# A two-layer transformer trunk on one core: the second MLP product by seven half-size products in place of eight

## The reference, cut to what matters

```python
# x: (1, 512, 1024) float32; D_FF = 4096; two layers
x = x + mixer(rmsnorm(x, g))               # attention, a different one in each layer
x = x + _mlp(rmsnorm(x, g), w1[i], w2[i])  # after each mixer
...
def _mlp(h, w1, w2):                       # w1: 1024 x 4096, w2: 4096 x 1024
    return jnp.square(jax.nn.relu(h @ w1)) @ w2
...
return _rmsnorm(x, norm_final)
```

## Time and profile before

| | |
|---|---|
| median of 3 runs | 1215.82 us (1214.65 to 1218.02) |
| the profiled execution | 1217.92 us |
| its span, first to last instruction | 1216.0 us |
| mean granted TensorE clock | 0.985 of full |
| PE busy | 96% (1166.2 us) |
| DVE, ACT, POOL busy | 56%, 42%, 43% |
| transfers | 104.94 MB, 86 GB/s on average |

### The profile page before, as it was taken

One profiled execution on the slowest core, in us unless ns is written; L12 is line 12 of the kernel. 1 busy time (PEld: TensorE's weight loads), 2 busy tenths in 40 slices (PEclk: granted clock), 3 DMA queues, 4 the chain that ended last, 5 costly groups with the idle time before them and its releaser, 6 DMA issues.

```text
span 1216.0 us, 15801 instructions
## 1 busy us (share of the span) xinstructions
PE 1166.2 (96%) x5601; PEld 959.6 (79%) x5605; DVE 678.5 (56%) x1094; ACT 505.6 (42%) x910; POOL 523.1 (43%) x267
## 2 busy tenths in 40 slices
PE   6999988999999999999997899989999999999997
PEld 4788877878888888888765677878788888888886
DVE  5867697664163163265669798737641541632654
ACT  6677665532132222225373387843322222221332
POOL 2433322444444444347643475224444444544441
PEclk9999989999999999999999999999999999999998
DMA  5233332333333333333322100103333333333331
GB/s 158 72 108 93 101 111 72 97 88 96 95 103 88 103 92 98 99 91 103 87 56 66 35 19 27 45 18 99 90 89 105 92 99 100 91 103 88 102 95 77
DMA packets 191225, 104.94 MB, mean 86 GB/s; under 512 B 9062, under 2 KB 187537, under 8 KB 191170
## 3 DMA queue, kind: packets, MB, share of 16 engines
q1 hardware_dynamic: 189900, 104.09, 29.8%
q10 hardware_dynamic: 1270, 0.13, 0.1%
HBM read 102.04 MB, written 6.35 MB: 89 GB/s over the span
## 4 chain that ended last, share of the span: by engine, by line
PE 81%; DVE 9%; ACT 5%; issue 3%; POOL 1%; DMA 1%; SPq 0%; ACTq 0%; DVEq 0%
PE bank L706 25%; PE bank L708 25%; PE bank L707 25%; ACT probs L1361 2%; PE bank L877 2%; DVE probT_l L1797 1%; POOL wl L1619 1%; PE bank L879 1%; PE bank L889 1%; ACT ur L1180 1%; PE bank L890 1%; DVE score L2118 1%; DVE probs L2020 1%; DMA score<-in_x 1%; ACT wh L1180 1%
## 5 line engine op out<-in xcount | busy, mean ns | idle before, releaser
L1619 POOL TENSOR_TENSOR wl<-raw,wh 128x1024 fp32r<-128x1024 f32 x171 | 417.9, 2445 | 549.1 <-ACT wh L1180 549.1
L706 PE MATMUL bank<-ur,wh 128*128 128x512 f32 x1072 | 418.6, 390 | 0.3 <-POOL wl L1619 0.3
L707 PE MATMUL bank<-ur,wh 128*128 128x512 f32 x1072 | 417.3, 389 | 0.0
L708 PE MATMUL bank<-ur,wl 128*128 128x512 f32 x1072 | 417.3, 389 | 0.0
L1180 ACT ACTIVATE wh<-raw 128x1024 fp32r<-128x1024 f32 x171 | 180.8, 1058 | 509.4 <-PE bank L708 509.0
L706 PEld LDWEIGHTS bank<-ur,wh 128*128 128x128 f32 x1072 | 201.5, 188 | 42.9 <-issue 1.6
L707 PEld LDWEIGHTS bank<-ur,wh 128*128 128x128 f32 x1072 | 201.4, 188 | 42.3 <-issue 0.5
L708 PEld LDWEIGHTS bank<-ur,wl 128*128 128x128 f32 x1072 | 201.4, 188 | 41.8
L1961 DVE TENSOR_TENSOR xT<-bank,xT 128x512 f32<-128x512 f32 x64 | 44.3, 692 | 227.6 <-PE bank L708 227.5
L1797 DVE TENSOR_TENSOR ur<-sq,ur 128x512 fp32r<-128x512 f32 x65 | 129.8, 1997 | 45.4 <-ACT ur L1180 45.4
L706 PE MATMUL bank<-xh,wh 128*128 128x512 f32 (+1 forms) x296 | 122.4, 413 | 8.9 <-DVE xl L1867 3.9
(11 more groups left out here) (221 smaller groups left out, 1293.7 us busy)
## 6 DMA issues: line engine op xcount, KB each, us to landing
raw<-in_w_mlp SPq DMA_DIRECT2D x128, 512.0 KB, 3.9
raw<-in_w_in_e SPq DMA_DIRECT2D x18, 512.0 KB, 3.7
raw<-in_w_in_o SPq DMA_DIRECT2D x10, 512.0 KB, 3.7
raw<-in_w_out_e SPq DMA_DIRECT2D x8, 512.0 KB, 3.8
raw<-in_w_out_o SPq DMA_DIRECT2D x8, 512.0 KB, 3.7
skew_c<-bias_rows SPq DMA_DIRECT2D x8, 319.5 KB, 4.5
strip_raw<-skew_c SPq DMA_DIRECT2D x8, 256.0 KB, 2.6
out<-probs SPq DMA_DIRECT2D x4, 512.0 KB, 2.6
```

The costliest lines, as they stand in the source:

```text
L706: mm(dst, lhs[0], rhs[0], start=start, stop=False, skip_group_check=not check)
L707: mm(dst, lhs[0], rhs[1], start=False, stop=False, skip_group_check=not check)
L708: return mm(dst, lhs[1], rhs[0], start=False, stop=stop, skip_group_check=not check)
L1619: return nc.gpsimd.tensor_tensor(dst, a, b, ALU.subtract)
```

## The change: what it does

In the first three groups of each MLP (`FAST = 3`) the second product is made by Strassen's scheme. The group's product (512 tokens x 1024 hidden features by 1024 x 1024) is cut in two in each direction. `h` gives four quarters of 512 hidden features x 256 tokens, W2 four quarters of 512x512 (`x`, `y`, `z`, where `z` is loaded twice, and each in two buffers of 128x1024). From the `h` quarters three more are made by sums and differences, so `combo_h` and `combo_l` hold seven combinations, four tiles each; the weight quarters are combined in place by four differences. Seven products of 512x512 by 512x256 follow, each of 48 matmuls with 128x128 weights and 256 moving columns. They accumulate in two pairs of banks (`z`, `v`), and after each product DVE adds the state of its pair into a quarter of `xT`. The fourth group of each layer is made as before.

The first product's slabs come in another order (tile 0, 4, 1, 5, ...), so that both halves of a pair are there early. DVE now takes a slab by one instruction (ReLU and scale, into `u_scaled`), ACT squares it, DVE makes the sums, ACT rounds the seven combinations and DVE makes their seven low parts. ACT rounds the weight combinations too, and DVE makes all their low parts. In these groups POOL only makes `wl` for the eight slabs of the first product. At the end there are four output buffers, and the transposes of features 0 to 511 stand ahead of the sum of squares.

```diff
+PRODUCTS = ((A11, "z", True, 0, "x", (0, 0)), (S1, "v", True, 1, "x", (1, 1)), (S2, "z", False, 2, "x", (0, 1)),
+            (S4, "v", False, 0, "z", (0, 1)), (S3, "z", False, 1, "y", (1, 1)), (A12, "v", True, 0, "z", (0, 0)),
+            (A22, "z", False, 1, "z", (1, 0)))
...
-        otok = praw[:, 0:2048].rearrange("p (a n) -> p a n", a=2)
+        otok = [praw[:, 0:1024], praw[:, 1024:2048], raw[:, 0, :], raw[:, 1, :]]
...  TensorE
+            def fast_group(layer, n0, norm, g):
+                G0 = FAST * layer
+                first_slabs(n0, norm, g)
+                for i, (c, pair, fresh, slot, _, _) in enumerate(PRODUCTS):
+                    pe.wait_ge(quarter_lo, HALVES * g + (HALVES * G0 + 2 * i + 2))
+                    if i < 3:
+                        pe.wait_ge(combo_lo, PARTS * g + (PARTS * G0 + (13, 15, 16)[i]))
+                    w = quarter_w[slot]
+                    for b in range(2):
+                        if i >= 2:
+                            pe.wait_ge(product_taken, BANKS_DONE * g + (BANKS_DONE * G0 + 2 * (i - 2) + b + 1))
+                        for d in range(2):
...
+                            for j in range(4):
...
+                                last = product(dst, (w[0][j // 2][:, cols], w[1][j // 2][:, cols]),
+                                               (combo_h[:, c, j, :], combo_l[:, c, j, :]), ...)
+                        last.then_inc(product_done, 1)
...
+            pe.wait_ge(slab_taken, N_END - 3)
+            pe.wait_ge(xg_hi, XG_BEFORE["final"] + 4)
+            for a in range(NQ):
+                turn_output(a, 0)
             pe.wait_ge(slab_taken, N_END)
             sum_squares("final")
...  ScalarE, group G, slab s
+                    if s + 2 < KT:
+                        split(n % 2, raw_count(n + 2), n + 1)
+                    act.wait_ge(slab_taken, n + 1)
+                    if s % 2 == 0:
+                        nc.scalar.activation(u_first[:, HS:3 * HS], u_scaled, ACT.Square).then_inc(u_ready, 1)
+                        act.wait_ge(sums_made, SUMS * G + 4 * j + 1)
+                        copy(combo_h[:, S3:A11 + 1, j, :], ...).then_inc(combo_hi, 1)
+                    else:
...  (the square, and three copies behind u_ready and sums_made)
+                    if s == 1:
+                        quarter_rounded(G, 0)
+                    if s == 4:
+                        quarter_rounded(G, 1)
...  VectorE, group G, slab s
+                    v.scalar_tensor_tensor(u_scaled, pj(n)[:, :], 0.0, rstd[:, :], ALU.max, ALU.mult).then_inc(slab_taken, 1)
+                    if s == 2:
+                        quarter_low(G, 0, 0)
+                    if s in (3, 4):
+                        quarter_sum(G, 0, s - 3)
+                    if s in (6, 7):
+                        quarter_sum(G, 1, s - 6)
+                    dve.wait_ge(u_ready, u + 1)
...  (one difference of 256 columns for even s, three for odd s)
+                    if s == 2:
+                        quarter_low(G, 0, 1)
+                    if s in (5, 6):
+                        quarter_low(G, 1, s - 5)
+                    if s == 7:
+                        quarter_sum(G, 2, 0)
...  (low parts: one of 512 columns for even s; 512, 256 and 512 for odd s)
```

More of the change, by code:

```diff
@@ L169, in trunk @@
         xT = sb("xT", [P, KT, S])
-        xh = sb("xh", [P, KT, S], F32R)
-        xl = sb("xl", [P, KT, S], F32R)
+        xhl = sb("xhl", [P, 2 * KT * S], F32R)
+        xh, xl = (xhl[:, KT * S * a:KT * S * (a + 1)].rearrange("p (k s) -> p k s", k=KT) for a in range(2))
         raw = sb("raw", [P, 2, 1024])
@@ L622, in load_mlp @@
-            def load_mlp(layer, n0):
-                with sp.Fori(0, GROUPS) as g:
-                    load_mlp_group(layer, n0, g)
+                for s in cols:
+                    n = n0 + KT * g + s
+                    sp.wait_ge(w_hi, n - 1)
+                    sp.wait_ge(w_lo, n - 1)
+                    tile = PAIR_ORDER[s] if g < FAST else s
+                    dst = raw[:, n % 2, :].rearrange("p (k n) -> p k n", k=KT)
+                    sp.dma_start(dst, w1[:, :, D * g + P * tile:D * g + P * (tile + 1)]).then_inc(raw_loaded[n % 2], 16)
@@ L779, in mlp, with turn_output, first_slabs @@
-            def mlp(n0, H0, norm):
-                mlp_group(n0, H0, norm, 0)
-                with pe.Fori(1, GROUPS) as g:
-                    mlp_group(n0, H0, norm, g)
+            def turn_output(a, half):
+                for k in range(4):
+                    last = nc.tensor.transpose(out_rows(a, half)[:, P * k:P * (k + 1)],
+                                               xT[:, 4 * half + k, P * a:P * (a + 1)], ident[:, :])
+                last.then_inc(fin_turned[half], 1)
+            def first_slabs(n0, norm, g):
+                for s in range(KT):
+                    n = KT * g + (n0 + s)
+                    pe.wait_ge(slab_taken, n - 3)
+                    wait = (lambda k: pe.wait_ge(xg_lo, XG_BEFORE[norm] + k + 1)) if s == 0 else None
+                    part = {0: lambda: sum_squares(norm), 1: lambda: spread(norm)}.get(s) if isinstance(g, int) and g == 0 else None
+                    slab(n, (n0 + s) % 2, pj(n0 + s)[:, :], xn, wait, norm_part=part, after=4 - s)
@@ new lines, in plain_group, with mlp @@
+            def plain_group(layer, n0, norm):
+                first_slabs(n0, norm, FAST)
+                for m in range(KT):
+                    n = n0 + KT * (FAST + 1) + m
+                    pe.wait_ge(slab_taken, n - 3)
+                    wait = (lambda k: pe.wait_ge(h_lo, KT * layer + k + 1)) if m == 0 else None
+                    slab(n, n % 2, pj(n)[:, :], hid, wait)
+            def mlp(layer, n0, norm):
+                fast_group(layer, n0, norm, 0)
+                with pe.Fori(1, FAST) as g:
+                    fast_group(layer, n0, norm, g)
+                plain_group(layer, n0, norm)
@@ L1305, in hidden, with quarter_rounded @@
                 copy(hid[0][:, slot, :], sq[:, slot % 2, :]).then_inc(h_hi, 1)
-            def mlp_group(n0, H0, g, norm=None, low=False):
+            def quarter_rounded(G, i):
+                _, _, _, slot, name, _ = PRODUCTS[i]
+                act.wait_ge(quarter_loaded[name], {"x": 32 * G + 32, "y": 32 * G + 32, "z": 64 * G + 32 * (1 + (i > 4))}[name])
+                made = (0, 2, 4, 0, 6, 0, 8)[i]
+                for half in range(2):
+                    if made:
+                        act.wait_ge(quarters_made, 8 * G + made - 1 + half)
+                    copy(quarter_w[slot][0][half], quarter[name][half]).then_inc(quarter_hi, 1)
@@ L1309, in mlp_group, with plain_group @@
+            def plain_group(layer, n0, norm, low):
                 for s in range(2 * KT):
-                    n = 16 * g + (n0 + s)
-                    if not isinstance(g, int) or n + 2 < N_END:
-                        split((n0 + s) % 2, raw_count(n + 2) if isinstance(g, int) else 128 * g + raw_count(n0 + s + 2),
-                              n + 1)
+                    n = n0 + KT * FAST + s
+                    if n + 2 < N_END:
+                        split(n % 2, raw_count(n + 2), n + 1)
@@ L1327, in mlp_group, with mlp @@
                                 copy(dst[0], src).then_inc(low_hi, 1)
-            def mlp(n0, H0, norm, following, low=False):
+            def mlp(layer, n0, norm, following, low=False):
                 root(norm)
-                with act.Fori(0, GROUPS - 1) as g:
-                    mlp_group(n0, H0, g)
-                mlp_group(n0, H0, GROUPS - 1, following, low)
+                for g in range(FAST):
+                    fast_group(layer, n0, g)
+                plain_group(layer, n0, following, low)
             def load_exp():
```

309 lines of the change are left out of this document (229 added, 80 removed).

## The result

The changed kernel takes 1226.34 us (median of 7 runs, 1222.36 to 1228.52) against 1218.02 us before, measured beside it: a ratio of 1.008, 95% interval 1.0063 to 1.0097.

The account below looks back on a forecast made before the run. The MLPs were taken as bound by the number and length of PE's matmuls. From 1217.9 us profiled: matmuls -26, stalls +38, clock +5, end -2 gave 1233, or 1231 in terms of the median; range 1203 to 1243.

Parts of the forecast that it names:

- rivals 2 and 3: 2: later products stall too, 1240 us, chance 0.15; 3: 256-column matmuls bound by weight load, 1330 us, chance 0.02.
- Rival 1: DVE keeps pace, so product 0's low part is ready at slab 7's end: 1188 us, half-way 1206; chance 0.2.
- Rival 4: All but nothing: 4 to 5 us of stall, no clock fall, 1213 to 1219 us; chance 0.08.
- The matmuls: Each fast group swaps 8 slabs for 336 matmuls of 256 columns at 0.1167 us, saving 4.3 us, 26 in all.
- The stalls: First half of each fast group: PE waits before slabs 4, 6, 7 and products 0, 1; 6.3 us, bounds 4.9 to 8.
- The turns of VectorE and POOL: DVE instructions with both operands in SBUF and POOL's never run side by side; if they could, stall would be 0.3 us.
- The clock: PE gaps before slab 7 and product 0 lower the clock; half of six falls at 1.7 us, +5, bounds 0 to 10.
- The second half: During the seven products DVE has 10 instructions of 1024 columns; low parts and weight quarters arrive in time, no stall.
- The end: After the last MLP, 16 early transposes and stores limited by DVE's scalings save 2 us; bounds 0 and 4.

Follow-up runs that it names:

- the kernel with short POOL instructions: Changed kernel with GpSimd making only 128 of 1024 columns of each low part of the first product's weights in the six fast groups; 1193.33 us, one run.
- the kernel with all spread anew: Changed kernel with first combinations made early for second and third groups, second combination rounded earlier, VectorE's pieces one or two slabs earlier; 1220.51 us, ratio 1.0034.
- the end alone: Kernel before with only four output buffers and 16 transposes ahead of the sum of squares; 1213.34 us, ratio 0.9981.
- early work: Changed kernel with the first weight combination of second and third fast groups made during product 6 of the group before; 1213.84 us, ratio 0.9979.
- ScalarE's move: Changed kernel with ScalarE rounding the second weight combination after slab 7's weights instead of before; 1214.35 us, ratio to the kernel before 0.9997.
- VectorE's move: Changed kernel with VectorE making the second combination's low parts after taking slab 7, its differences behind slab 7; 1212.04 us, ratio to the kernel before 0.9966.
- the kernels with both moves: Changed kernel with ScalarE rounding the second combination later and VectorE's low parts and differences for it later; three variants, 1202.73, 1201.79 and 1200.78 us.

## Why the prediction was right, point by point

- **The direction and the mechanism.** Less matmul time, more stall, on the two places named; right. No stall between the products; right, and rivals 2 and 3 did not come. Rival 1 (it decides from 4.6 us of stall a group) was nearer than I held it: the stalls were 4.36 us, but the matmuls saved less too. Rival 4 had the stalls right, with its 4 to 5 us; what it lacked were the 7 us of the matmuls.
- **The matmuls**, -4.3 us a group: mis-sized, -3.2. I took 0.1167 from five starts that were rounded to 0.01 us; the bound of 0.12 was the truth, and 336 of them make the difference of 1.1 us a group, 7 in all. A short row of starts gives no third digit. The Trainium skill ("TensorE: Matmul & The Clock Gate", section "Back-to-back issue gap") gives columns/2.4 plus 2.5 ns, 109 ns for 256, as the gap of an isolated matmul; the prediction held it against dense rows without saying so. The dense rows of these traces lie above it: 120 ns for 256 and 226.7 for 512 columns, both 32 clock cycles of 2.4 GHz over the column count, for matmuls that each have their own float32 weights.
- **The stalls**, +6.3 us a group: mis-sized, +4.36, under the lower bound of 4.9. By place: slab 7 1.76 (forecast 2.4), product 0 2.06 (3.25), slab 4 0.25 (0.35), slab 6 none (0.2), product 1 none (0.13), and 0.3 in second matmuls behind the gaps, for which I had no term. The durations were right. What failed was laying them end to end: consecutive DVE instructions whose data is there start 0.08 us before the record of the one before ends (1.22 us of record, 1.13 to 1.14 apart), and forty instructions stand between slab 0's end and `combo_lo` 13. In the third group 26 of them start so, 2.1 us in all, where 1.9 lie between forecast and trace. That no other error of the table stands behind these 1.9 is argued, not shown. The two errors, +7 us of the matmuls and -12 of the stalls, partly cancelled, and that the time came within 5 us of the forecast is in part that luck.
- **The turns of VectorE and POOL**: right, by 2.92 and 3.12 us for instructions that take 1.21 alone, and by the kernel with short POOL instructions. The Trainium skill's rule ("SBUF — State Buffer", section "SBUF: two separate sides") holds here in both directions. DVE waits for POOL: the same instruction takes 2.17 us behind a running `wl` and 0.43 without. POOL waits for DVE: in the kernel with all spread anew a `wl` that starts at 263.15, 0.04 us behind a DVE instruction of 0.42, lasts 2.62 us in place of 2.40. The takes, which read PSUM, last 0.68 us beside POOL as without it.
- **The clock**, +5 us: mis-sized, 1.5. One group of six had the fall, though all have the same two gaps. What tells that one from the five stays open.
- **The second half**: no stall, right. But its count was short: behind slab 7 DVE has 13 instructions of 1024 columns, not 10. And weight quarters did not land faster than the 3.9 us of a slab's weights, as I took them to: by the buffer that they go to, the medians are 3.8 to 7.0 us. Neither cost anything.
- **The end**, -2: it was -2.6 in the traces and -2.3 in the runs of the end alone. That a part of it is the clock of the sum itself was not in the forecast.
- **In the sum** 1233 was forecast for the profiled execution and 1227.4 came: matmuls +7, stalls -12, clock -3.5, end -0.6, and +3.5 in stretches for which I had no term (until the first MLP 1.4, between the MLPs 1.3, the rest of the MLPs 0.8). The trace of the end alone, which is the kernel before in all these stretches, has 1.2 and 1.5 in the first two, so they differ from one execution to the next and are not the change's.
- **What I did not see** before the experiments: that both stalls can be taken away by order alone, with all the load in place. Less load does it too, on POOL, on VectorE, or for slab 7 by early work. The forecast had the two ScalarE copies ahead of `wh` and wrote the stall's price down, but never asked where else they could stand.

## What to carry to other kernels

When a change trades matmul time for work on the other engines, lay that work out against the engine that waits, and for each stall ask what stands ahead of the late instruction that nobody needs yet; here two moves of work that was not due, without an instruction less, turned +0.8% into -1.1 to -1.3%. Where two engines take turns and the stretch is full, move work behind the point that is waited for, not within it: here the spreading within the half cost 7 us. And take a matmul's distance from dozens of starts, since a fixed part of 32 cycles doubles its share when the columns are halved.

## What the runs showed of the hardware that was not expected

- A matmul with 256 moving columns and its own float32 weights costs 0.120 us in a dense row, 512 columns 0.2267; halving the columns costs 6%, 20.5 us over 64 slabs.
- The records of DVE and ACT instructions overlap in a dense row by 0.08 to 0.09 us (DVE 1.22 us of record and 1.13 to 1.14 of spacing; ACT 1.04 and 0.95), so a sum of records is too long.
- POOL's low part of 128 columns has records of 0.46 and 0.95 us, and that of 1024 columns 2.40.
- Gaps of PE of the same length at the same place bring a clock fall in one group and none in the next (changed kernel: in the first of six; ScalarE's move: in the second and in the last; VectorE's move, with one gap of 1.6 us a group: in none; the kernels with both moves, whose gaps are at most 0.4 us of idle time: in none).
